# Down projections of two feed-forwards as seven half-width block products on one Trainium2 core

## The reference

```python
def swiglu(h, w_gate, w_up, w_down):                     # block 1
    return (jax.nn.silu(h @ w_gate) * (h @ w_up)) @ w_down

def _conv_glu(h, w_up, conv_w, conv_b, w_down):          # block 2
    u = _causal_dwconv(h @ w_up, conv_w) + conv_b
    gate, up = jnp.split(u, 2, axis=-1)
    return (jax.nn.silu(gate) * up) @ w_down
```

## Time and profile before

| | |
|---|---|
| median of 3 runs | 1654.82 us (1653.6 to 1656.62) |
| profiled execution, its own time | 1653.65 us |
| its span | 1651.9 us |
| PE busy | 1636.7 us, 99% |
| PE weight load busy (overlaps PE) | 1321.6 us, 80% |
| DVE busy | 881.9 us, 53% |
| ACT busy | 664.8 us, 40% |
| POOL busy | 142.0 us, 9% |

### The profile page before, as it was taken

The page is one execution under the profiler, slowest core; times in us unless marked ns, Lnnn a source line. Parts: engine busy times, 40 slices in busy tenths (PEclk is TensorE's granted clock), DMA queues, the critical chain, the costliest instruction groups (busy, mean ns, idle before and its releaser), DMA issues.

```text
span 1651.9 us, 19032 instructions
## 1 busy us (share of the span) xinstructions
PE 1636.7 (99%) x7732; PEld 1321.6 (80%) x7732; DVE 881.9 (53%) x1169; ACT 664.8 (40%) x974; POOL 142.0 (9%) x164
## 2 busy tenths in 40 slices
PE   9999999999999999999999999999999999999999
PEld 7788878888878778888888877877767788888887
DVE  5446754554754454444443336766555677777321
ACT  5353334333553343322223325256684544444211
POOL 0000001211210010000000210312111100000000
PEclk9999999999999999999999999999999999999999
DMA  7222222323454123332333332422213232332331
GB/s 260 97 83 73 87 91 72 94 90 102 166 165 127 40 78 93 97 101 91 102 96 97 101 102 90 145 99 65 65 64 116 82 109 91 102 99 93 102 99 54
DMA packets 47462, 164.33 MB, mean 99 GB/s; under 512 B 5056, under 2 KB 5184, under 8 KB 47056
## 3 DMA queue, kind: packets, MB, share of 16 engines
q1 hardware_dynamic: 46192, 158.88, 29.9%
q0 software_dynamic: 896, 3.70, 0.7%
q10 hardware_dynamic: 288, 0.54, 0.1%
HBM read 158.88 MB, written 4.23 MB: 99 GB/s over the span
## 4 chain that ended last, share of the span: by engine, by line
PE 95%; DVE 2%; ACT 2%; issue 1%; DMA 0%; POOL 0%; SPq 0%; DVEq 0%; ACTq 0%; POOLq 0%
PE pst L426 93%; PE pst L886 1%; PE pst L594 1%; DVE XL L1662 0%; ACT WH L1005 0%; DVE WL L1650 0%; DMA raw<-wst 0%; ACT L1010 0%; DVE qx L1894 0%; ACT misc L1005 0%; POOL acc L2382 0%; PE pst L716 0%; DVE ML L1658 0%; DVE X L1874 0%; ACT XH L1005 0%
## 5 line engine op out<-in xcount | busy, mean ns | idle before, releaser
L426 PE MATMUL pst<-XH,WH 128*128 128x512 f32 x1312 | 523.2, 399 | 1.3 <-DVE WL L1650 0.6
L426 PE MATMUL pst<-XH,WL 128*128 128x512 f32 x1312 | 511.7, 390 | 0.0
L426 PE MATMUL pst<-XL,WH 128*128 128x512 f32 x1312 | 511.4, 390 | 0.0
L1650 DVE TENSOR_TENSOR WL<-raw,WH 128x1024 fp32r<-128x1024 f32 x275 | 338.9, 1233 | 318.0 <-ACT WH L1005 317.6
L1005 ACT ACTIVATE WH<-raw 128x1024 fp32r<-128x1024 f32 (+1 forms) x277 | 289.9, 1049 | 325.1 <-PE pst L426 318.5
L426 PEld LDWEIGHTS pst<-XH,WH 128*128 128x128 f32 x1312 | 246.6, 188 | 62.2 <-issue 11.5
L426 PEld LDWEIGHTS pst<-XL,WH 128*128 128x128 f32 x1312 | 246.8, 188 | 52.3 <-issue 2.6
L426 PEld LDWEIGHTS pst<-XH,WL 128*128 128x128 f32 x1312 | 246.5, 188 | 52.4
L426 PE MATMUL pst<-HH,WH 128*128 128x512 f32 x352 | 136.9, 389 | 0.0
L426 PE MATMUL pst<-HL,WH 128*128 128x512 f32 x352 | 136.9, 389 | 0.0
L426 PE MATMUL pst<-HH,WL 128*128 128x512 f32 x352 | 136.9, 389 | 0.0
(11 more groups left out here) (274 smaller groups left out, 1783.9 us busy)
## 6 DMA issues: line engine op xcount, KB each, us to landing
raw<-wst SPq DMA_DIRECT2D x276, 512.0 KB, 3.5
X<-xT SPq DMA_DIRECT2D x7, 512.0 KB, 7.8
xs<-X SPq DMA_DIRECT2D x1, 2048.0 KB, 9.2
nC<-cd POOLq DMA_DIRECT2D x4, 512.0 KB, 8.1
X<-xs SPq DMA_DIRECT2D x2, 1024.0 KB, 5.5
outT<-X SPq DMA_DIRECT2D x8, 256.0 KB, 4.4
qx<-memT SPq DMA_DIRECT2D x1, 1024.0 KB, 4.9
gt<-cd POOLq DMA_DIRECT2D x1, 1024.0 KB, 8.8
```

What stands on the lines that cost most here:

```text
L426: return nc.tensor.matmul(out, lhs, rhs, start=start, stop=stop)
L1650: vec.tensor_tensor(WL[:, i % NHL, :], raw[:, i % NRAW, :], WH[:, i % NHL, :].bitcast(F32), ALU.subtract).then_inc(wl, 1)
```

## The change

Each down projection is computed with seven products of half-size blocks instead of eight (the Strassen-Winograd scheme). The two halves of the token dimension (256 columns each), the even and odd hidden tiles, and the even and odd output tiles make the 2 x 2 x 2 split. The products are `p1` to `p7`.

- **Products.** For each output pair `mp` (4 of them) the products come in the order `p1, p5, p7, p6, p4, p3, p2` (`MP_SEQ`), each over all hidden pairs of the phase, three matmuls of 256 columns per pair. `p2` is added in the bank of `p1`, `p6` in that of `p5`, `p4` in that of `p7`, so that each of them waits until ACT or DVE has taken the earlier content out (`copied`, `evicted`).
- **Two phases.** The hidden tiles are no longer all kept. Up tiles 0 to 11 are followed by 28 products over 6 pairs (`PAIRS`), then up tiles 12 to 21 by 28 products over 5 pairs. There are 4 x 7 x 2 x 2 = 112 products and 4 x 7 x (6 + 5) x 3 x 2 = 1848 matmuls of 256 columns in the place of 1056 of 512.
- **Activation sums.** For each pair of hidden tiles DVE forms four differences and sums of 256 columns (`combine`), ACT rounds seven slots of 256 columns into `TH` (`pair_hi`) and DVE forms `TL` (`pair_lo`). In the first pair of a phase (mp = 0) the last hidden pair of `p7` and `p6` is taken after the others of both.
- **Weight sums.** Four weight planes per feed-forward (2.88 MB each) are sums of weight blocks. They are made in DRAM: SP copies a plane in four pieces (`copy_in`), POOL issues a DMA that adds another plane (`sum_in`). SP's copies stand between weight loads at fixed chunks, two of them wait for earlier sums.
- **Chunks.** A down chunk is one product's weights: 128 x 768 in the first phase, 128 x 640 in the second; 112 of them replace 44 of 128 x 1024.
- **Output.** Per output pair and phase ACT copies `p1` and `p5` to `ev`; DVE does eight additions, seven of 256 columns and one of 512, into `X`, `y`.

The core of the diff:

```diff
+MP_SEQ = [(m, p) for m in range(4) for p in ("p1", "p5", "p7", "p6", "p4", "p3", "p2")]
+TILES = (range(0, 12), range(12, HID))
...
-                flat = 0
-                for m in range(8):
-                    b = ring()
-                    free(b)
-                    for k in range(HID):
...
-                        ins = mm3(ps[b][:, :], h[:, un, :], l[:, un, :], HH[:, k, :], HL[:, k, :], k == 0, k == HID - 1)
...
+                def product(mp, prod, ks):
+                    g, b = 8 * (which - 1) + 4 * ph + mp, down_bank(mp, prod)
+                    if ks[0] == 0:
+                        got[mp, prod] = [units(w) for w in chunk(f"ffn_down{which}")]
+                        if prod == "p2":
+                            pe.wait_ge(*copied(g, 0))
+                        elif prod == "p6":
+                            pe.wait_ge(*copied(g, 1))
+                        elif prod == "p4":
+                            pe.wait_ge(*evicted(g, 0))
...
+                    for k in ks:
+                        pe.wait_ge(hl, paired(which, 2 * (PAIRS[ph][0] + k)) + (2 if prod in ("p1", "p5") else 4))
+                        ins = mm3(ps[b][:, 0:256], h[:, k, :], l[:, k, :], TH[:, k, t], TL[:, k, t], not more and k == 0, k == n - 1, more)
...
+                for mp, prod in MP_SEQ:
+                    if (mp, prod) == (0, "p7"):
+                        product(0, "p7", range(n - 1))
+                        product(0, "p6", range(n - 1))
+                        product(0, "p7", range(n - 1, n))
+                        product(0, "p6", range(n - 1, n))
+                    elif (mp, prod) != (0, "p6"):
+                        product(mp, prod, range(n))
...
+                for x, (mp, prod) in enumerate(MP_SEQ):
+                    g = 8 * (which - 1) + 4 * ph + mp
+                    if x:
                         chunk()
...
+                    if x == 2:
+                        pair_lo(which, TILES[ph][-1])
...
+            def sum_in(which, to, plane, ready):
+                pool.wait_ge(xs_out, 256 * (which - 1) + ready)
...
+                gp.dma_start(rows_[0], rows_[1], accum_op=ALU.add, max_dma_last_dim=8192).then_inc(eg_in, 16)
...
+            load_to("wk_xa", 2, 5)
+            copy_in(1, 2, sums[0][0], 32)
+            load_to("wq_xa", 0, 5)
+            copy_in(1, 3, sums[0][2], 48)
```

More of the change, by code:

```diff
@@ L205, in program @@
         cd = nc.dram_tensor("cd", [16, T], F32, kind="Internal").ap()
+        wd = [wd1, wd2]
+        sums = [nc.dram_tensor(f"sums{n}", [4, PLANE_N], F32, kind="Internal").ap() for n in (1, 2)]
         sty = ExitStack()
@@ L767, in pe_program, with ffn @@
+            def ffn(which):
+                for ph in range(2):
+                    ups(which, TILES[ph])
+                    down(which, ph)
             ffn(1)
@@ L785, in put @@
                 b = bank2() if b is None else b
-                for x, _ in enumerate(tile(name, b, XH, XL, ready=ready, cuts=cuts)):
+                for x, _ in enumerate(tile(name, b, XH, XL, ready=ready, cuts=cuts, ks=FINAL_ORDER)):
                     if x == 1:
@@ L795, in heads_main @@
                 chunk("gate2")
-                for k in range(8):
-                    pe.wait_ge(x_add, 16 + k + 1)
+                for k in FINAL_ORDER:
+                    pe.wait_ge(*final(1, k))
                     part = slice(32 * (k % 4), 32 * (k % 4) + 32)
@@ L1345, in after1 @@
+                for ph in range(2):
+                    ups(TILES[ph])
+                    down(ph)
+            def after1(n):
+                m = FINAL_ORDER[n]
+                act.wait_ge(*final(1, m))
                 act.wait_ge(mm_, DONE["ffn_up1", 43])
@@ L1994, in bank2 @@
+            for ph in range(2):
+                ups1(TILES[ph])
+                if ph:
+                    dve.wait_ge(once, 3)
+                down(1, ph, after1)
+                at["ring"] = 2
             def bank2():
@@ L2534, in load, with copy_in @@
                             sp.wait_ge(wl, i - NRAW + 2)
-                        nc.sync.dma_start(raw[:, i % NRAW, :], wst[i]).then_inc(raw_in[i % NRAW], 16)
+                        name, j = PLAN[i]
+                        if not name.startswith("ffn_down"):
+                            nc.sync.dma_start(raw[:, i % NRAW, :], wst[at["main"]]).then_inc(raw_in[i % NRAW], 16)
+                            at["main"] += 1
+                            continue
+                        ph, mp, prod = DOWN[j]
+                        w = int(name[-1]) - 1
+                        made, plane = PLANE[prod]
+                        if made:
+                            sp.wait_ge(eg_in, 64 * (w + 1))
+                        part, n = plane_slice(ph, mp)
+                        src = (sums if made else wd)[w][plane, part].rearrange("(p c) -> p c", c=n)
+                        nc.sync.dma_start(raw[:, i % NRAW, 0:n], src).then_inc(raw_in[i % NRAW], 16)
+            def copy_in(which, to, src, ready=None):
+                if ready:
+                    sp.wait_ge(eg_in, 64 * (which - 1) + ready)
+                rows_ = [a.rearrange("(r c) -> r c", c=1024) for a in (sums[which - 1][to], src)]
+                for x in range(4):
+                    nc.sync.dma_start(rows_[0][176 * x:176 * x + 176], rows_[1][176 * x:176 * x + 176]).then_inc(xs_out, 16)
+                    load()
             def load_to(name, i, ahead):
```

439 lines of the change are left out of this document (291 added, 148 removed).

## The result

The changed kernel takes 1655.19 us (median of 12 runs, 1654.02 to 1660.09), beside 1653.78 (12 runs of before, 1650.89 to 1656.62) on the same chip. The ratio is 1.0016, 95% interval [1.0008, 1.0023]: a loss of some 0.16%, small but clear of zero, where a gain of 0.7% was forecast. The profiled execution took 1654.02 us itself, its span is 1651.9, the span of before.

The account below looks back on a forecast made before the run. PE was taken as the bound, busy 1636.7 of 1651.9 us. Products -17.8, phase starts +6.2, ends -0.6 give -12.2 on 1653.65, so 1641.45; the median lies 1.2 above, say 1643 us; 8 in 10 range 1627 to 1656.

Parts of the forecast that it names:

- third rival: The rival "the gain is given back beside PE": 1647 to 1656 us, chance 0.14.
- within 0.2%: Case that the time cannot be told from no change, about 3.3 us either way; chance 0.08.
- The products: PE in the down stages: 256-column matmuls come p = 120 ns apart, 221.8 us for 239.6, a saving of 17.8 us.
- surplus by columns: Rival, PE in down stages: the 13.6 ns surplus grows with the columns, p 111 to 115 ns, 1631 us; chance 0.24.
- loads bound: Rival, PE in down stages: weight loads bound short matmuls, slower above p = 126.6 ns, 1768 us at 188 ns; chance 0.12.
- The four phase starts: PE waits at each phase's start for the last odd hidden tile and p4's bank: 6.2 us, bounds 3 and 10.
- The up stage of the second block: DVE's added combining steps and low parts there are hidden by its waits: costed at nothing, up to 9 us.
- Ends: The final addition is 256 columns, 0.42 us for 0.70, twice: -0.6 us.
- What lies beside PE: DVE and ACT work during the products fits with a chunk of slack, DVE 10.8 us in 12.6: no cost.
- the 7.4 us of the norm stays: The norm's 7.4 us, from 986.7 to 994.06 us, was to remain unchanged.
- The weight sums: Copies and adding DMAs in DRAM: the tight third sum has 26 us; cost nothing to 4 us, 0 taken.
- the gain is given back beside PE: Rival: DVE in the second up stage (9 us), or SP behind a slow sum (4 and more); chance 0.14.

Follow-up runs that it names:

- e4: Changed kernel with p1 and p5 of the second output pair taken before p7 of the first; 1653.22 us, 0.9992 of before.
- e3: Changed kernel with POOL's fourteen additions of squares in the first block on 8 columns instead of 512; 1643.90 us, 0.9935 of before.
- e1: Changed kernel without weight sums and their copies, all products reading the planes of `wd` as they are; 1650.42 us, 0.9980 of before.
- e2: Changed kernel with the third and fourth copies of the first feed-forward moved later, to the query projections; 1652.56 us, 0.9991 of before.
- e12: e6 with six buffers of squares, a tile's two squares added in one instruction of 1024 columns, one tile later; 1642.95 us, 0.9933 of before.
- e7: Kernel before, with only the 14 additions of squares moved from POOL to DVE; 1650.51 us, 0.9988 of before.
- e5: Changed kernel with the first block's 14 additions of squares on DVE instead of POOL; 1652.84 us, 0.9997 of before.
- e6: Changed kernel with the edits of e2, e4 and e5 together; 1644.44 us, 0.9952 of before.
- e8: Changed kernel with the edits of e4 and e5, copies left where they are; 1648.38 us, 0.9975 of before.
- e11: e6 with four buffers of squares, a tile's two squares added at once in one instruction of 1024 columns; 1642.14 us, 0.9933 of before.
- e9: Changed kernel with the edits of e2 and e4, POOL's additions of squares left where they are; 1646.75 us, 0.9960 of before.

## Why the prediction was wrong

1643 with "faster" at 0.79 was forecast, and 1655 came: inside the range only because that reached to the edge of the third rival, and on the case "within 0.2%" that had 0.08. By its own steps:

- **The products**: right. The distance p is 119.9 ns for 120, the saving 17.8 us as forecast. The 13.3 ns on top of the 106.7 belong to each matmul and do not grow with the columns. The 28 ns that the prediction took from the Trainium skill ("TensorE: Matmul & The Clock Gate", "Back-to-back issue gap") for 128 columns, and that would have given an estimated 135 ns, are not there at 256 columns of fp32r. The same section has some 131 ns for 512 columns, which the prediction left out; here they take 226.7. The rivals "surplus by columns" and "loads bound" fall with it.
- **The four phase starts**: right in place and size, 5.2 us for 6.2 (0.64, 1.12, 1.22, 2.22 for 0.45, 0.95, 1.95, 2.85); e4 shows that half of them can be had back.
- **The up stage of the second block**, costed at nothing: right. PE waits nowhere between 1312 and 1420 nor between 1495 and 1590 us. **Ends**: right, 0.42 for 0.70.
- **What lies beside PE**: here it failed, twice. "Both fit, with a chunk of slack" added up DVE's instructions at the durations they have alone, 10.8 us in each 12.6. POOL's additions of squares were named, but only as late, several stages off; fourteen of them fall into this very phase, and each holds up a DVE instruction by up to 1.1 us. The step's own warning came true (PE waits directly for a late chunk), for 3.4 us. And "the 7.4 us of the norm stays" was wrong by 3.7: two tiles of an output pair are now finished at the same time, so four squares queue for POOL at the end instead of two, 7.31 us for 3.86. e3 takes away both and what POOL's additions cost in the norm before, 9.4 us in all.
- **The weight sums**: the interval "nothing to 4 us" was set with the time that a sum may take (26 us; it took some 20), and 0 was chosen. The sum was in time; what was missed is that it and the copies fill the DMA engines for some 70 us, so that the ordinary weight loads beside them land late. It cost some 5 us (e1 5.9, e2 4.1). SP did wait for a sum once, 9.4 us near 712 us, and PE did not feel it.

The sum with what was measured: -17.8 + 5.2 - 0.6 + 5.2 + 3.4 + 3.7 = -0.9 us. The matmuls just behind each wait come late as well, 1.4 us in all, and 0.9 us are won near 1300 us, where nothing was changed: -0.4. The spans of the two profiles are equal to 0.1 us, and the ratio says +1.3 to +3.8. The rival "the gain is given back beside PE" (0.14, 1647 to 1656) named the outcome and SP behind a slow sum, but put DVE's part in the second up stage, where there was none.

Open: the 2.5 us near 466 us. The addition on POOL meets the low part in some profiles of the same code and not in others (PE's wait there is 2.7 us in the changed kernel, e2, e3 and e12, and in e7, which has nothing of the change, 1.6 in before, e1, e4, e5, e6 and e8 to e11), so it belongs to the execution, not to the change; no run here fixes it. Where the loads are the limit behind it (changed kernel, e3 to e5, e8), the start of the up stage is 4.8 to 6.6 us late with it or without it, so there the whole 5.2 us are the price of the loads. What e1 gains beyond e2 (1.8 us) is within what the runs can tell.

## What to carry to other kernels

When a change makes PE's products shorter, add up the engines beside it again phase by phase, and for DVE with the durations that its two-input instructions have while POOL is at work, not those they have alone. Look at what finishes together at a stage's end: the way through the norm behind it is a chain over ACT, DVE and POOL with few buffers, and a pair of tiles that is finished together doubles the additions at its tail (3.86 to 7.31 us on POOL here). And a transfer that is in time for its own reader can still be in the way of all others: place bulk copies where the DMA share is low. With the three repairs (copies later, starts interleaved, squares added by DVE from four buffers) the kernel is nearly the 12 us faster that were forecast, 0.9933 of before, [0.9921, 0.9946]; some 2 of its 11 us are had without the change, by moving the additions to DVE alone (e7).

## What the runs showed that was not expected

- A DVE instruction with two SBUF inputs beside an addition of 512 columns on POOL (1.56 us) takes up to 1.1 us longer; one with an operand in PSUM runs through at 0.41 us.
- The same wait of PE costs more in one execution than in another. In e2 the 60 matmuls behind it took 8.95 us with a granted clock of 0.70 on the mean of 6 us, in the changed kernel 7.46 us at 1.00. In e9, behind the same wait, the clock was at 0.50, the 1.2 GHz level, for 3.2 us; so it was in e11 behind the norm, PE having been idle for 3.2 us:

```profile
988.00:994.00 6.00, 5.66 (x13) 4.45 (x14) 3.42 (x5) 4.34 (x6) 0.00 (x0) 0.50 0.56 175
```

- At the 1.2 GHz level nothing comes on top of the columns: behind the wait in e9 fourteen matmuls of 256 columns come 213 ns apart, and near 470 us in the changed kernel matmuls of 512 columns come 427 ns apart (256 and 512 columns at 1.2 GHz are 213.3 and 426.7). At the 2.4 GHz level it is 13.3 ns at either width.
- A DMA that adds 2.88 MB from DRAM to DRAM lands after 20.1 us (median of 8), a plain copy of 0.7 MB after 6 to 7. The Trainium skill, "DMA: Bandwidth & Descriptors", section "Queues, rings and completion order", says that a DMA engine takes turns between its queues packet by packet. The weight loads that land after 10.9 to 16.6 us beside the sum alone, which is on another queue than theirs, fit that; no run separates it from a limit of the memory that both read.
